# Attention on one core: score product ahead of the first value product, value bank copied first, mask and bias added on GpSimd in the sparse heads

## The chip, the cores and the metric

The kernel runs on 1 core of one Trainium2 chip. The metric is the time of one execution on the device in microseconds. Before the change the median of 3 runs is 1541.96 us (1541.03 to 1543.17).

## The reference

One layer of a hybrid encoder for 1,024 tokens plus 16 meta tokens (L = 1040), model width 1024, all in float32: a projection, two attention branches, a mixture of experts, norms. The change lies in the attention. Branch A has 8 dense heads, masked by chunks of 64 tokens. Branch B has 8 sparse heads: an indexer picks 256 keys for each query, and a relative bias (T5 buckets) is added before the softmax.

```python
# branch A, per block of 128 queries
s = (einsum('bqhd,bkhd->bhqk', qn, k_nope) + einsum('bqhr,bkr->bhqk', qr, k_rope)) * scale_a
s = where(cid[None, :] <= chunk_ids(pq)[:, None], s, NEG_INF)
o_a = einsum('bhqk,bkhd->bqhd', softmax(s), v_a)
# branch B, per block of 128 queries
score = einsum('bqh,bqhk->bqk', wb, relu(einsum('bqhd,bkd->bqhk', qib, k_i)))
_, idx = top_k(where(cid <= cq, score, NEG_INF), 256)
s = einsum('bqhd,bqkhd->bhqk', qb, gather(k_b, idx)) * scale_b
s = s + rel_bias[t5_bucket(idx - pq)]
s = where(valid, s, NEG_INF)
o_b = einsum('bhqk,bqkhd->bqhd', softmax(s), gather(v_b, idx))
```

The kernel gathers nothing: for the sparse heads it computes all scores of a block and adds a mask (0 or -1e30, bf16) that was made earlier from the indexer's scores.

## The kernel before

**Tiling.** The attention stage runs from about 547 to 899 us of the span. Queries come in 8 blocks of 128 rows; block i sees 16 + 128 (i + 1) keys, so its width WID[i] is 144, 272, 400, 528, 656, 784, 912 or 1040. Each of the 16 heads (0 to 7 dense, 8 to 15 sparse) is two super-steps: the even one handles blocks 0, 1, 2, 3 and the odd one blocks 4, 5, 7, 6 (`ORDER`), so the 1040 block comes before the 912 block. Super-step s holds block number g = 4 s + position; s >= 16 is sparse.

**Work of a block.** TensorE computes the scores (`qk`, f32 split in a high and a low part: three products in a dense head; in a sparse head one product of the identity with the mask, L1140, then two, L1143 and L1145), into one of two score areas in PSUM. VectorE takes the row maximum (`row_max`): in a dense head a reduction (L1285), in a sparse head one operation that adds the relative bias `tb`, writes the sum to `sbias` and gives the maximum (L1278), then a small negation (L1282). ScalarE takes the exponential (`exp`, L1227) into `px`.

**Work of a turn.** A super-step has turns, in an order written out by hand in `turns`: 5 (even) or 9 (odd) "p" turns, one for each tile of 128 keys; a "q" turn at index 5 that finishes the super-step before; and, in two of every four super-steps (s % 4 of 0 or 1), an "o" turn at index 2, which transposes finished outputs. In a "p" turn TensorE transposes `px` into a bank (L1187), ScalarE copies it rounded to `pH` (L1239), VectorE subtracts for the low part `pL` (L1302), and three turns later TensorE multiplies both with the values into the value bank, bank 7 (`pv`, L1203, L1204). `qk_after` says behind which turn the score product of a coming block is issued: index 0, 1, 3 of an even super-step (blocks 5, 7, 6 of the next), index 0, 1, 3, 5, 8 of an odd one (blocks 0 to 3 of the next, and block 4 of the one after). All engines keep this order: TensorE does turn, `pv`, `qk`; VectorE the subtraction, then `row_max`; ScalarE the copy, then the exponential of the block issued one turn earlier.

**The value bank.** It holds one super-step's sum. After its last `pv` (at turn index 2 of the next super-step, or 1 behind an even one without an "o" turn) ScalarE copies it to `oT` (L1251, semaphore `s_ot`); the first `pv` of the next super-step (turn index 3) waits for `s_ot`. In an "o" turn ScalarE also copies the output bank (L1243, to `OaT` or `ObT`), before the value bank.

**GpSimd** (`values`, `queries`, `keys`, `scaled`) splits values, queries and keys of coming heads in high and low parts and scales finished outputs (L1322), in this order: at odd s values, queries, scaled; at even s keys, scaled. `scaled(s - 1)` waits for VectorE's `otmp` (L1309, the "q" turn). **SP** loads queries, keys, the bias `tb` (two buffers) and values of the sparse heads; the load of `tb` for head h waits with `s_mx` for all maxima of head h - 2.

Of the kernel before, what the change touches and what calls it, by code (L numbers as in the profile page):

```python
# [88 lines left out]
def hybrid_layer(nc, a, out):  # L89

    ctx = ExitStack()
    with ctx:
# [905 lines left out]
        tb = [at(f"tb{k}", [P, L], F32, (R_Q + 8192, R_V + 8320)[k]) for k in range(2)]  # L998
        VR = [at(f"VR{k}", [P, 9, HD], F32, (R_Q + 12352, R_V + 12480)[k]) for k in range(2)]
# [79 lines left out]
        def bank_of(k):  # L1079
# [3 lines left out]
         s_vr) = map(sem, ["s_qk", "s_mx", "s_ml", "s_ex", "s_t", "s_ld", "s_rs", "s_pv", "s_ot", "s_qa", "s_rc",  # L1083
                           "s_om", "s_oe", "s_z", "s_vz", "s_hs", "s_hr", "s_vl", "s_vr"])

        with block() as blk:
            @blk.sync
            def _(sp):
                for h in range(H):
                    j, u, k, hh = h // 2, h % 2, h % 2, H + h  # L1090

                    sp.wait_ge(s_hr, 6 if h < 2 else 2 * (hh - 2) - 1)
                    for dup in range(2):
                        sp.dma_start(QR[k][64 * dup:64 * (dup + 1), :], qb_d[j, 64 * u:64 * (u + 1), :]
                                     ).then_inc(s_qr[k], 16)
                    if h >= 2:
                        sp.wait_ge(s_hr, 2 * (hh - 2))
                    for dup in range(2):
                        sp.dma_start(KR[k][64 * dup:64 * (dup + 1), :], kb_d[j, 64 * u:64 * (u + 1), :]
                                     ).then_inc(s_kr[k], 16)  # L1100
                    if h == 1:
                        sp.wait_ge(s_vr, 2 * H)
                    if h >= 2:
                        sp.wait_ge(s_mx, 8 * (h - 1))
                    sp.dma_start(tb[k][:, :], skewed[h]).then_inc(s_tb[k], 16)
                    if h >= 2:
                        sp.wait_ge(s_vr, 2 * (hh - 1))
                    c = slice(HD * h, HD * (h + 1))
                    sp.dma_start(VR[k][:, 0:8, :], vb_d[0:T, c].rearrange("(t p) c -> p t c", p=P)
                                 ).then_inc(s_vd[k], 16)  # L1110
                    sp.dma_start(VR[k][0:META, 8, :], vb_d[T:L, c]).then_inc(s_vd[k], 16)
                    if h == 1:
                        sp.wait_ge(s_hr, 2 * (H - 1))
                        for piece in range(2):
                            load_branch_weights(sp, piece, s_wb)

            @blk.tensor
            def _(pe):
                def qk(g):
# [17 lines left out]
                    if sparse(s):  # L1137
                        q = QS[hh % 2][:, own]
                        for lo, hi in parts:
                            pe.matmul(flat[:, o + lo:o + hi], identb[:, :], mask[:, OFF[i] + lo:OFF[i] + hi],  # L1140
                                      start=True, stop=False)
                        for lo, hi in parts:
                            pe.matmul(flat[:, o + lo:o + hi], q, kh[:, lo:hi], start=False, stop=False)  # L1143
# [65 lines left out]
                for k in range(len(turns)):  # L1209
                    turn(k)  # L1210
                    for n in pv_after[k]:
                        pv(n)
                    if k in qk_after:
# [3 lines left out]
            def _(act):  # L1217
# [14 lines left out]
                for k in range(len(turns)):  # L1232
# [7 lines left out]
                    elif kind == "o":  # L1240
                        act.wait_ge(s_t, k + 1)
                        to, j = (ObT, s // 4 - 4) if sparse(s) else (OaT, s // 4)
                        act.copy(to[:, j, 512 * (s % 2):512 * (s % 2 + 1)], bank_of(k)).then_inc(s_oe, 1)  # L1243
                    for before in pv_after[k]:
# [6 lines left out]
                        act.copy(oT[done % 2][:, :], ps[:, 7, :]).then_inc(s_ot, 1)  # L1251
                    if k - 1 in qk_after:
# [3 lines left out]
            def _(dve):  # L1256
# [4 lines left out]
                def row_max(g):  # L1261
# [8 lines left out]
                    if sparse(s):  # L1270
# [7 lines left out]
                        dve.tensor_tensor_reduce(sbias[g % 2][:, 0:w], flat[:, o:o + w], tb[h % 2][:, c:c + w],  # L1278
# [35 lines left out]
            def _(pool):  # L1314
# [55 lines left out]

                for k in range(2):
# [4 lines left out]
                for s in range(NSS):  # L1376
# [9 lines left out]
                    if s >= 1:  # L1386
                        scaled(s - 1)
                scaled(NSS - 1)
# [1089 lines left out]
```

## Time and profile before

| | us |
|---|---|
| median of 3 runs | 1541.96 |
| lowest, highest | 1541.03, 1543.17 |
| the profiled execution's own time | 1541.31 |
| its span | 1539.5 |
| TensorE (PE) busy | 1372.2 |
| VectorE (DVE) busy | 1031.2 |
| ScalarE (ACT) busy | 666.5 |
| GpSimd (POOL) busy | 420.2 |

The profile is one execution. PE is the matmul part of TensorE, PEld its loading of weights. A row of the timeline gives the start in us from the span's start, the duration, engine, line of the code, operation and the tiles it writes and reads; in brackets stands how long the engine had been idle and what ended that. "issue" means that nothing the profile shows released it.

### The profile page before, as it was taken

To read this page: it belongs to the slowest core of one execution; us is meant where nothing else is said; L and a number is where in the kernel's file an instruction comes from. 1 tells how busy PE (TensorE), PEld (TensorE's weight loads), DVE (VectorE), ACT (ScalarE), POOL (GpSimd) and SP (SyncE) were. 2 spreads that over 40 slices of the span, in tenths; PEclk is the share of its full clock that TensorE was granted. 3 is DMA by queue.
4 is the path that set the end of the run, shared out by engine and by line. 5 is a ranking of instruction groups with operands and counts; after the bars stand their busy time and mean duration, and the time that the engine had idled before them with its cause. 6 is when DMAs were issued, how large, how long until landed. Compare 5 with 4: busy or idle time off the path is not lost. (4 is left out here: it accounts for less than half of the span.)

```text
span 1539.5 us, 21819 instructions
## 1 busy us (share of the span) xinstructions
PE 1372.2 (89%) x7326; PEld 1120.2 (73%) x7327; DVE 1031.2 (67%) x1950; ACT 666.5 (43%) x1179; POOL 420.2 (27%) x476
## 2 busy tenths in 40 slices
PE   6989999999999989998888879999828999999950
PEld 4779788789989567777777768899726777777730
DVE  4458999999940856677777754433357777777727
ACT  5357323312211356666666651112106666666622
POOL 1100334412121044445544214200021233333213
PEclk9999999999999989999999989999858999999985
DMA  6040411132232003003442054222176999999718
GB/s 202 28 151 23 147 56 48 62 103 76 97 101 82 4 1 77 1 1 104 98 97 70 1 164 155 92 100 77 70 308 221 350 357 349 361 376 377 290 45 325
DMA packets 88702, 217.40 MB, mean 141 GB/s; under 512 B 24784, under 2 KB 49904, under 8 KB 76328
## 3 DMA queue, kind: packets, MB, share of 16 engines
q1 hardware_dynamic: 77200, 190.45, 35.7%
q0 software_dynamic: 9216, 16.80, 3.0%
q10 hardware_dynamic: 2200, 9.02, 1.5%
q8 instruction: 52, 0.85, 0.2%
q14 instruction: 34, 0.28, 0.1%
HBM read 193.05 MB, written 44.73 MB: 154 GB/s over the span
## 5 line engine op out<-in xcount | busy, mean ns | idle before, releaser
L421 PE MATMUL ps<-hHi,g_lead 128*128 128x512 f32 (+2 forms) x480 | 184.5, 384 | 7.8 <-DVE g_rest L818 6.6
L315 DVE TENSOR_SCALAR_CACHE_REDUCE mask<-score,cand 128x272 bf16<-128x272 f32 (+6 forms) x224 | 185.5, 892 | 4.6 <-DVE cand L334 4.4
L1302 DVE TENSOR_TENSOR pL<-ps,pH 128x512 fp32r<-128x512 f32 (+3 forms) x224 | 126.8, 573 | 89.2 <-ACT pH L1239 86.6
L2211 DVE TENSOR_TENSOR w_rest<-wgu,w_lead 128x1024 fp32r<-128x1024 f32 x128 | 155.9, 1222 | 45.1 <-ACT w_lead L2158 43.7
L422 PE MATMUL ps<-hLo,g_lead 128*128 128x512 f32 (+2 forms) x480 | 183.7, 383 | 0.0
L423 PE MATMUL ps<-hHi,g_rest 128*128 128x512 f32 (+2 forms) x480 | 182.5, 380 | 0.0
L2158 ACT CAST w_lead<-wgu 128x1024 fp32r<-128x1024 f32 x128 | 134.4, 1055 | 37.8 <-PE ps L2104 37.8
L1239 ACT CAST pH<-ps 128x512 fp32r<-128x512 f32 (+3 forms) x224 | 107.0, 492 | 70.9 <-PE ps L1187 70.7
L732 POOL TENSOR_TENSOR g_rest<-g_raw,g_lead 128x2048 fp32r<-128x2048 f32 x12 | 55.6, 4631 | 299.5 <-ACT g_lead L588 299.5
L2102 PE MATMUL ps<-w_lead,x_lead 128*128 128x512 f32 x256 | 114.0, 445 | 6.0 <-DVE w_rest L2211 6.0
L2124 PE MATMUL ps<-wd,hmT 128*128 128x512 f32 x256 | 115.3, 593 | 1.6 <-DVE hmT L2234 1.0
L1203 PE MATMUL ps<-pH,VS 128*128 128x512 f32 (+3 forms) x224 | 96.0, 429 | 17.7 <-issue 17.7
L421 PEld LDWEIGHTS ps<-hHi,g_lead 128*128 128x128 f32 x480 | 90.8, 189 | 24.8 <-issue 7.0
L423 PEld LDWEIGHTS ps<-hHi,g_rest 128*128 128x128 f32 x480 | 91.0, 190 | 16.6
L2104 PE MATMUL ps<-w_lead,x_rest 128*128 128x512 f32 x256 | 101.8, 398 | 0.0
L422 PEld LDWEIGHTS ps<-hLo,g_lead 128*128 128x128 f32 x480 | 90.8, 189 | 14.8
L2103 PE MATMUL ps<-w_rest,x_lead 128*128 128x512 f32 x256 | 100.8, 394 | 0.0
L2064 POOL DMA_INDIRECT ys_d<-ye,dk x32 | 32.3, 1010 | 213.1 <-DVE ye L2246 204.3
L2124 PEld LDWEIGHTS ps<-wd,hmT 128*128 128x128 f32 x256 | 46.2, 190 | 47.8 <-issue 47.8
L1204 PE MATMUL ps<-pL,VS 128*128 128x512 f32 (+3 forms) x224 | 79.5, 355 | 0.0
L1322 POOL TENSOR_TENSOR otok<-otmp,rec 128x256 f32<-128x256 f32 x32 | 19.6, 613 | 187.0 <-DVE otmp L1309 182.2
L619 ACT ACTIVATE stage<-ps 128x512 f32<-128x512 f32 x32 | 19.1, 598 | 112.0 <-PE ps L423 112.0
(349 smaller groups left out, 3433.2 us busy)
## 6 DMA issues: line engine op xcount, KB each, us to landing
wgu<-in_w_exp_gate SPq DMA_DIRECT2D x32, 1024.0 KB
wgu<-in_w_exp_up SPq DMA_DIRECT2D x32, 1024.0 KB
wd<-in_w_exp_down SPq DMA_DIRECT2D x32, 1024.0 KB, 11.7
g_raw<-in_w_in SPq DMA_DIRECT2D x16, 1024.0 KB, 5.6
gates_d<-stage SPq DMA_DIRECT2D x32, 256.0 KB, 2.0
gt<-gates_d SPq DMA_DIRECT2D x32, 256.0 KB, 3.1
rel_d<-rel_s ACTq DMA_DIRECT2D x1, 4672.0 KB
KR<-kb_d SPq DMA_DIRECT2D x16, 260.0 KB, 6.3
```

The source lines that it names most:

```text
L315: return dve.tensor_scalar(mask[:, OFF[i]:OFF[i + 1]], score[:, OFF[i]:OFF[i + 1]], thr, 0.0, op, ALU.add, accum_out=cnt[:, i:i + 1])
L421: pe.matmul(dst, x[0], y[0], start=(k == 0), stop=False)
L422: pe.matmul(dst, x[0], y[1], start=False, stop=False)
L423: return pe.matmul(dst, x[1], y[0], start=False, stop=(k == KT - 1))
L1239: act.copy(pH[n % RING][:, lo:512], bank_of(k)[:, lo:512]).then_inc(s_ld, 1)
L1302: dve.tensor_tensor(pL[n % RING][:, lo:512], bank_of(k)[:, lo:512], pH[n % RING][:, lo:512].bitcast(F32), ALU.subtract).then_inc(s_rs, 1)
L2102: pe.matmul(dst, xl[:, k, :], wl, start=(k == 0), stop=False)
L2103: pe.matmul(dst, xl[:, k, :], wr, start=False, stop=False)
L2104: mm = pe.matmul(dst, xr[:, k, :], wl, start=False, stop=(k == KT - 1))
L2124: mm = pe.matmul(ps[:, 5 + half, :], hmT[u % 2][:, k, :], wd[u][:, k, 512 * half:512 * (half + 1)], start=(k == 0), stop=(k == 1))
L2158: act.copy(w_lead[part][:, :, :, :], wgu[u][:, :, 2 * part:2 * part + 2, :]).then_inc(S["m_wl"], 1)
L2211: dve.tensor_tensor(w_rest[u][:, :, 2 * part:2 * part + 2, :], wgu[u][:, :, 2 * part:2 * part + 2, :], w_lead[part][:, :, :, :].bitcast(F3 ...
```

## The change

On TensorE, at a turn after which the first `pv` of a super-step stands (turn index 3), the score product is issued ahead of that `pv` instead of behind it. On ScalarE the copy of the value bank comes before the copy of the output bank. In the sparse heads the six blocks 2 to 7 (`JOINED`) have no mask product; GpSimd adds the block's mask (bf16) and relative bias (f32) into a tile `joined[i]` of its own, and VectorE's maximum reads that instead of `tb`. Blocks 0 and 1 stay as they are. The additions of super-step s + 2 stand at the end of GpSimd's work for super-step s: blocks 2 and 3 at even s, 4, 5, 7, 6 at odd s. SP's load of `tb` now waits for two maxima and all six additions of the head two before.

```diff
--- before.py
+++ after.py
@@ -996,6 +996,9 @@
         QS = [at(f"QS{k}", [P, T], F32R, R_Q + 4096 * k) for k in range(2)]
         sbias = [at(f"sbias{k}", [P, L], F32, R_V + 4160 * k) for k in range(2)]
         tb = [at(f"tb{k}", [P, L], F32, (R_Q + 8192, R_V + 8320)[k]) for k in range(2)]
+        JOINED = (2, 3, 4, 5, 7, 6)
+        joined = {i: at(f"tbm{i}", [P, WID[i]], F32, R_Q + 14656 + 4 * sum(WID[2:i])) for i in JOINED}
+        assert 14656 + 4 * sum(WID[2:]) <= 32768
         VR = [at(f"VR{k}", [P, 9, HD], F32, (R_Q + 12352, R_V + 12480)[k]) for k in range(2)]
         wbr = [at(f"wbr{k}", [P, 2, 4, 256], F32, R_K + 16640 + 8192 * k) for k in range(2)]
 
@@ -1080,8 +1083,8 @@
             return ps[:, bank_no[k], :]
 
         (s_qk, s_mx, s_ml, s_ex, s_t, s_ld, s_rs, s_pv, s_ot, s_qa, s_rc, s_om, s_oe, s_z, s_vz, s_hl, s_hr, s_vl,
-         s_vr) = map(sem, ["s_qk", "s_mx", "s_ml", "s_ex", "s_t", "s_ld", "s_rs", "s_pv", "s_ot", "s_qa", "s_rc",
-                           "s_om", "s_oe", "s_z", "s_vz", "s_hs", "s_hr", "s_vl", "s_vr"])
+         s_vr, s_jn) = map(sem, ["s_qk", "s_mx", "s_ml", "s_ex", "s_t", "s_ld", "s_rs", "s_pv", "s_ot", "s_qa", "s_rc",
+                           "s_om", "s_oe", "s_z", "s_vz", "s_hs", "s_hr", "s_vl", "s_vr", "s_jn"])
 
         with block() as blk:
             @blk.sync
@@ -1101,7 +1104,8 @@
                     if h == 1:
                         sp.wait_ge(s_vr, 2 * H)
                     if h >= 2:
-                        sp.wait_ge(s_mx, 8 * (h - 1))
+                        sp.wait_ge(s_mx, 8 * (h - 2) + 2)
+                        sp.wait_ge(s_jn, 6 * (h - 1))
                     sp.dma_start(tb[k][:, :], skewed[h]).then_inc(s_tb[k], 16)
                     if h >= 2:
                         sp.wait_ge(s_vr, 2 * (hh - 1))
@@ -1136,11 +1140,11 @@
                     kh, kl = KH[hh % 2], KL[hh % 2]
                     if sparse(s):
                         q = QS[hh % 2][:, own]
-                        for lo, hi in parts:
+                        for lo, hi in parts if i not in JOINED else ():
                             pe.matmul(flat[:, o + lo:o + hi], identb[:, :], mask[:, OFF[i] + lo:OFF[i] + hi],
                                       start=True, stop=False)
                         for lo, hi in parts:
-                            pe.matmul(flat[:, o + lo:o + hi], q, kh[:, lo:hi], start=False, stop=False)
+                            pe.matmul(flat[:, o + lo:o + hi], q, kh[:, lo:hi], start=i in JOINED, stop=False)
                         for lo, hi in parts:
                             mm = pe.matmul(flat[:, o + lo:o + hi], q, kl[:, lo:hi], start=False, stop=True)
                     else:
@@ -1208,9 +1212,12 @@
                     qk(g)
                 for k in range(len(turns)):
                     turn(k)
+                    opens = any(turns[n][2] == 0 for n in pv_after[k])
+                    if opens and k in qk_after:
+                        qk(qk_after[k])
                     for n in pv_after[k]:
                         pv(n)
-                    if k in qk_after:
+                    if not opens and k in qk_after:
                         qk(qk_after[k])
 
             @blk.scalar
@@ -1237,10 +1244,6 @@
                         if n >= RING:
                             act.wait_ge(s_pv, n - RING + 1)
                         act.copy(pH[n % RING][:, lo:512], bank_of(k)[:, lo:512]).then_inc(s_ld, 1)
-                    elif kind == "o":
-                        act.wait_ge(s_t, k + 1)
-                        to, j = (ObT, s // 4 - 4) if sparse(s) else (OaT, s // 4)
-                        act.copy(to[:, j, 512 * (s % 2):512 * (s % 2 + 1)], bank_of(k)).then_inc(s_oe, 1)
                     for before in pv_after[k]:
                         done = turns[before][1]
                         if turns[before] != last_tile(done):
@@ -1249,6 +1252,10 @@
                         if done >= 2:
                             act.wait_ge(s_t, turn_of[("q", done - 2, 0)] + 1)
                         act.copy(oT[done % 2][:, :], ps[:, 7, :]).then_inc(s_ot, 1)
+                    if kind == "o":
+                        act.wait_ge(s_t, k + 1)
+                        to, j = (ObT, s // 4 - 4) if sparse(s) else (OaT, s // 4)
+                        act.copy(to[:, j, 512 * (s % 2):512 * (s % 2 + 1)], bank_of(k)).then_inc(s_oe, 1)
                     if k - 1 in qk_after:
                         exp(qk_after[k - 1])
 
@@ -1275,7 +1282,11 @@
                             dve.wait_ge(s_tb[h % 2], 16 * (h // 2 + 1))
                             dve.wait_ge(s_vr, 2 * H)
                         c = P * (NB - 1 - i)
-                        dve.tensor_tensor_reduce(sbias[g % 2][:, 0:w], flat[:, o:o + w], tb[h % 2][:, c:c + w],
+                        add = tb[h % 2][:, c:c + w]
+                        if i in JOINED:
+                            dve.wait_ge(s_jn, 6 * h + JOINED.index(i) + 1)
+                            add = joined[i][:, :]
+                        dve.tensor_tensor_reduce(sbias[g % 2][:, 0:w], flat[:, o:o + w], add,
                                                  1.0, -3.0e38, ALU.add, ALU.max,
                                                  top[:, g % 2:g % 2 + 1]).then_inc(s_mx, 1)
                         dve.wait_ge(s_mx, g - 8 * H + 1)
@@ -1368,6 +1379,20 @@
                     pool.tensor_tensor(KL[k][0:rows_k, :], raw, KH[k][0:rows_k, :].bitcast(F32),
                                        ALU.subtract).then_inc(s_hr, 1)
 
+                def join(s):
+                    h, first = s // 2 - H, 4 * s - 8 * H
+                    if s == 2 * H:
+                        pool.wait_ge(s_hr, 2 * H)
+                    if s % 2 == 0:
+                        pool.wait_ge(s_tb[h % 2], 16 * (h // 2 + 1))
+                    for j, i in enumerate(ORDER[s % 2]):
+                        if i in JOINED:
+                            if h:
+                                pool.wait_ge(s_mx, first - 8 + j + 1)
+                            c = P * (NB - 1 - i)
+                            pool.tensor_tensor(joined[i][:, :], mask[:, OFF[i]:OFF[i + 1]], tb[h % 2][:, c:c + WID[i]],
+                                               ALU.add).then_inc(s_jn, 1)
+
                 for k in range(2):
                     pool.memset(VS[k][:, 8, :].bitcast(F32), 0.0).then_inc(s_vz, 1)
                 pool.wait_ge(s_vz, 2)
@@ -1385,6 +1410,8 @@
                         keys(hh + 1)
                     if s >= 1:
                         scaled(s - 1)
+                    if 2 * H <= s + 2 < NSS:
+                        join(s + 2)
                 scaled(NSS - 1)
 
         with block() as blk:
```

## Rows read from the trace of the kernel before

**Rows 1.** The page: busy time of each engine, its share of the span, and instructions.

```profile
PE 1372.2 (89%) x7326; PEld 1120.2 (73%) x7327; DVE 1031.2 (67%) x1950; ACT 666.5 (43%) x1179; POOL 420.2 (27%) x476
```

**Rows 2.** Stretches of two heads: dense, then sparse. Per engine: busy us (instructions), granted clock, DMA.

```profile
608.20:650.30 42.10, 38.48 (x269) 33.06 (x269) 29.45 (x52) 28.18 (x67) 20.57 (x21) 1.00 0.09 20
778.50:821.50 43.00, 37.60 (x253) 31.04 (x253) 31.37 (x84) 28.87 (x67) 20.62 (x21) 1.00 0.37 87
```

**Rows 3.** Timeline of sparse heads: start us, us, engine, line, operation; in brackets the wait before.

```profile
789.37 0.83 DVE L1278 CUSTOM_DVE_ANT_0 sbias<-ps,tb 128x656 f32<-128x656 f32 x1
...
810.56 0.83 DVE L1278 CUSTOM_DVE_ANT_0 sbias<-ps,tb 128x656 f32<-128x656 f32 x1
...
815.34 1.23 DVE L1278 CUSTOM_DVE_ANT_0 sbias<-ps,tb 128x1040 f32<-128x1040 f32 x1
...
816.96 0.47 PE L1203 MATMUL ps<-pH,VS 128*128 128x512 f32 x1 [0.93 <-issue]
...
818.46 0.56 DVE L1302 TENSOR_TENSOR pL<-ps,pH 128x384 fp32r<-128x384 f32 x1 [1.69 <-ACT pH L1239]
...
818.93 1.10 DVE L1278 CUSTOM_DVE_ANT_0 sbias<-ps,tb 128x912 f32<-128x912 f32 x1
...
820.26 1.05 ACT L1227 ACTIVATE pxb<-sbias,negm 128x912 f32<-128x912 f32 x1 [0.75 <-DVE negm L1282]
...
820.48 0.68 DVE L1309 TENSOR_REDUCE otmp<-ps 128x256 f32<-128x512 f32 x1
...
821.46 0.66 PE L1187 MATMUL ps<-con,pxb 128*128 128x128 f32 x4 [0.99 <-ACT pxb L1227]
```

**Rows 4.** Timeline of dense heads.

```profile
610.79 0.62 PE L1187 MATMUL ps<-con,pxa 128*128 128x128 f32 x4
...
611.99 0.47 PE L1203 MATMUL ps<-pH,VS 128*128 128x512 f32 x1 [0.57 <-issue]
...
624.00 1.24 DVE L1285 TENSOR_REDUCE negm<-ps 128x1 f32<-128x1040 f32 x1 [0.41 <-PE ps L1154]
...
627.46 1.11 DVE L1285 TENSOR_REDUCE negm<-ps 128x1 f32<-128x912 f32 x1 [0.25 <-PE ps L1154]
...
644.64 0.28 PE L1204 MATMUL ps<-pL,VS 128*128 128x128 f32 x1
...
644.78 0.58 ACT L1243 COPY OaT<-ps 128x512 f32<-128x512 f32 x1 [0.21 <-PE ps L1191]
```

**Rows 5.** Timeline, TensorE, the 912 block's three products and what follows.

```profile
796.38 0.56 PE L1140 MATMUL ps<-mask,identb 128*128 128x456 bf16 x2
...
797.60 0.27 PE L1187 MATMUL ps<-con,px 128*128 128x128 f32 x1
```

**Rows 6.** Groups of instructions of GpSimd in two sparse heads: busy us, mean ns.

```profile
L1368 POOL TENSOR_TENSOR KL<-KR,KH 128x1040 fp32r<-128x1040 f32 x2 | 4.8, 2424 | 0.2
...
L1339 POOL TENSOR_TENSOR VS<-VR,VS 128x512 fp32r<-128x512 f32 x2 | 2.6, 1284 | 0.2
L1366 POOL CAST KH<-KR 128x1040 fp32r<-128x1040 f32 x2 | 2.1, 1052 | 0.0
```

**Rows 7.** Timeline of GpSimd in a sparse head.

```profile
778.25 0.61 POOL L1322 TENSOR_TENSOR otok<-otmp,rec 128x256 f32<-128x256 f32 x1 [9.33 <-DVE otmp L1309]
778.81 0.61 POOL L1336 CAST VS<-VR 128x512 fp32r<-128x512 f32 x1
...
782.28 2.39 POOL L1355 TENSOR_TENSOR QS<-QR,QS 64x1024 fp32r<-64x1024 f32 x1
...
799.98 0.61 POOL L1322 TENSOR_TENSOR otok<-otmp,rec 128x256 f32<-128x256 f32 x1 [9.60 <-DVE otmp L1309]
```

**Rows 8.** VectorE's negation, all of them, and one beside GpSimd's work.

```profile
L1282 DVE TENSOR_SCALAR negm<-top x64: 153/154/156, 716.3 to 884.9; 128x1 f32<-128x1 f32 x64
...
809.50 2.41 POOL L1368 TENSOR_TENSOR KL<-KR,KH 128x1040 fp32r<-128x1040 f32 x1
...
811.43 0.15 DVE L1282 TENSOR_SCALAR negm<-top 128x1 f32<-128x1 f32 x1
```

## The prediction

> **What bounds the kernel now.** I began with the page: TensorE is busy for 89% of the span and GpSimd for 27% [rows 1]. Shares of a whole span say little of one stage, so the second view is the table of stretches, cut at the start of an odd super-step, which repeats every two heads. Two dense heads take 42.1 us with TensorE busy 38.48; two sparse heads take 43.0 us with TensorE 37.60, VectorE 31.37, ScalarE 28.87 and GpSimd 20.62 [rows 2]. TensorE is the busiest everywhere and still idles 5.4 us in two sparse heads. Whether it decides is a question of order, not of shares, so the third view is the timeline, read backwards from one wait to what ended it.
>
> In a sparse head I start from the transposes that open an odd super-step: at 821.46 TensorE had waited 0.99 us for the exponential of block 6 (912 columns). That exponential (820.26) waited for VectorE's negated maximum, the row maximum (818.93) stood right behind the low-part subtraction (818.46), which had waited 1.69 us for ScalarE's high-part copy, and that copy comes, in ScalarE's order, behind the exponential of the 1040 block, whose maximum ran at 815.34 [rows 3]. So it goes on: maximum, exponential, copy, subtraction, next maximum, handed between VectorE and ScalarE, each in its written order. TensorE enters the chain once a head, with the four transposes at 821.46. Its score product is not in it: it waited 0.93 us at 816.96 for the value bank's copy, and the row maximum was still held by the subtraction.
>
> In a dense head the maximum is a plain reduction, with no negation of its own, and TensorE comes into the chain: the maximum of the 1040 block had waited 0.41 us for TensorE at 624.00, and that of the 912 block 0.25 us at 627.46 [rows 4].
>
> **Part 1: the score product ahead of the first value product.** At turn index 3 of every super-step the score product goes before the value product that waits for s_ot. In the dense heads TensorE stood 0.57 us at 611.99, between an odd super-step with an output turn and the even one behind it [rows 4]. The transposes ahead of that wait started at 610.79 and need about 0.4 us to issue, so the score product can start at about 611.2, up to 0.79 us earlier. The next place where the chain is seen waiting for TensorE is the 1040 block's maximum, which has 0.41 us of such a wait: the gain is between 0.41 and 0.79. I take 0.65, because copies and subtractions before it wait for TensorE too. The 912 block's maximum gains its 0.25 as well, since its product now ends early. Together 0.90 in each of the three dense pairs that have this (super-steps 5/6, 9/10, 13/14), and 0.25 once at super-step 2: -2.95 us. In the sparse heads the same swap fills a 0.93 us idle and gives nothing, because the work behind it was not waiting for TensorE. No DMA is moved by this part.
>
> **Part 2: the value bank copied before the output bank.** On ScalarE the order is output copy, value copy, exponential. The two copies cost the same in either order, unless the value bank is not ready. At an even dense super-step with an output turn the last value product ends at 644.64 + 0.28 = 644.92 while the output copy could start at 644.78 [rows 4]. ScalarE now stands for about 0.17 us, and what is queued behind it are both copies and the 1040 exponential, hence the chain. Three such places: +0.5 us. The dense net of parts 1 and 2 is -2.45 us, or between -1.7 and -2.9 with the bounds above.
>
> **Part 3: six mask products out, six additions in.** Removed from TensorE: the bf16 products of mask and identity in the six blocks above 272 columns, 4,320 columns a head. The three products of the 912 block (2,736 columns) started at 796.38 and the next transposes at 797.60 [rows 5], 0.446 ns a column; so 1.93 us a head, 15.4 us over eight heads. By the chain above this is worth nothing: VectorE's reduction has the same width, ScalarE's exponential the same, and the products were not late. VectorE gets one more wait per maximum, which costs nothing while the maximum stands behind a subtraction.
>
> Added to GpSimd: six additions a head, bf16 plus f32 to f32. No such operand pair is in the trace. Nearest are the f32 subtractions: 1.284 us for 512 columns and 2.424 for 1040 [rows 6], so 0.18 us and 2.16 ns a column. That gives 1.04, 1.32, 1.59, 1.87, 2.42 and 2.15 us for 400, 528, 656, 784, 1040 and 912, 10.4 us a head. GpSimd goes from 10.3 to 20.7 of 21.5 us. Below, a one-input cast of 1040 columns took 1.05 us [rows 6], so the additions can't be under 43% of my price. Above, the dearest f32 work of two inputs is this same row, and a conversion could add to it; I allow 20% more and take the f32 price.
>
> Now the order on GpSimd. Inside an even super-step a scaling starts at 799.98, right after VectorE's otmp. Behind it now come 400 and 528 (0.56 for the scaling, 2.26 with the 0.05 overlap of each), then values and queries, which ran from 778.81 to 782.28 + 2.39 = 784.67, 5.86 us, a gap of 0.07, the second scaling 0.56, then 656, 1.59 us, and 0.06 to VectorE [rows 7]. The joined 656 block is there at 799.98 + 10.96 = 810.94. The row maximum that reads it ran at 810.56 [rows 3]: 0.38 late. In the other kind of odd super-step (with an output turn) GpSimd starts at 778.25, the block is there at 789.21, and the maximum ran at 789.37: in time by 0.16. After the 656 block, 1040 was needed 4.8 us later (815.34) and comes 4.2 after it; 912 and the keys' split end 9.9 us after it, and otmp for the next scaling ended at 820.48 + 0.68, 10.6 after it [rows 3]. So four of eight odd super-steps are late by 0.38: +1.5 us. Queued behind the late maximum is the whole VectorE-ScalarE chain.
>
> The DMA side: SP's load of the relative bias waited for the last maximum of the head two before; it now waits for two maxima and six additions of it, which end some 2 us earlier, and queries and keys of the next head, behind it on SP, are needed a head later. Nothing.
>
> VectorE and GpSimd side by side: 64 negations took 153 to 156 ns each, and the one at 811.43 ran in the middle of a 2.41 us GpSimd subtraction begun at 809.50 [rows 8]. The Trainium skill (SBUF - State Buffer, Who interferes with whom) says that VectorE's f32 single-input operations in their two-port modes and GpSimd lock one another out for a whole instruction. By that rule GpSimd at 96% would hold up each negation; by the row it would not. The row decides, so the sum has nothing for it.
>
> **The sum.** -2.45 + 1.5 = -0.9 us. The profiled execution took 1541.31 us for its span of 1539.5; the median of the runs is 1541.96, 0.65 above it, and the difference carries over: 1541.1 us.
>
> **Rivals.**
> *A: the additions are in time.* With a price 25% under mine nothing is late: -2.45, at most -2.9, 1539.1 to 1539.5 us.
> *B: GpSimd sets the pace (the other side).* Before a 656 block 1,584 columns of additions stand, after it 2,736. For each 10% on their price the first makes 0.34 us, with slacks of -0.38 and 0.16, and the second 0.59 with a slack of about 0.65. At +20% two heads lose 1.06 + 0.52 + 2 x 0.53 = 2.6 us, ten over eight heads: 1541.96 - 2.45 + 10.5 = 1550 us. From about +13% the kernel is slower by over 0.2%. For it speaks that GpSimd is left with 0.8 us a head; against it that the price of two f32 inputs is steady in the trace.
> *C: TensorE decides after all.* Then the mask columns count in full: -15.4 us, 1526.6 us, and the filled waits on top. For it: TensorE is busiest; against it: rows 3. The Trainium skill (Perfetto Trace Analysis, Identifying the Most-Contended Engine) says to improve the engine with the highest occupancy first; by that rule this would be the result.
> *D: the lock.* If each of eight negations a head waited half a mean addition (0.87 us), 7 us a head: 1597 us.
>
> **Chances.** Forecast 0.47, A 0.20, B 0.22, C 0.07, D 0.04. What this measurement can tell is 0.2%, 3.1 us. A ends close above that bound and a dense gain a little larger crosses it: Faster gets half of A, all of C and 0.08 of the forecast's own spread, 0.25; slower gets B but its mild 0.05, D and 0.01 of the forecast, 0.22; within, 0.53. The range leaves out C, D and the far end of B: 1537.5 to 1549.0 us.
>
> **What would show it.** Right: two sparse heads stay at 42.5 to 44 us though TensorE's busy time falls by 3 to 4; before every second 656 maximum VectorE waits 0.3 to 0.5 us for GpSimd; the value product's waits are gone in both halves; two dense heads take about 41.4 us. Wrong: sparse heads well under 42 us (then C), GpSimd additions over 1.15 times my prices (B), negations over 0.2 us apart from the work ahead (D), or dense heads unchanged.

## The result, and the profile after

The changed kernel takes 1546.48 us (median of 8 runs, 1544.02 to 1549.28) beside 1542.07 us (8 runs) for the kernel before on the same chip: a ratio of 1.0028, 95% interval 1.0018 to 1.0037. It is slower by 4.4 us; the forecast was 0.9 us faster. Measured again later it came out at 1.0016 (1.0007 to 1.0025), so the loss is 2.5 to 4.4 us. The profiled execution took 1546.49 us, its span is 1544.6.

The page, in its busy row and two of its groups (busy us, mean ns, idle before):

```profile
PE 1367.7 (89%) x7230; PEld 1116.0 (72%) x7231; DVE 1029.8 (67%) x1950; ACT 664.8 (43%) x1179; POOL 493.2 (32%) x524
...
L1313 DVE TENSOR_TENSOR pL<-ps,pH 128x512 fp32r<-128x512 f32 (+3 forms) x224 | 126.8, 572 | 92.8 <-ACT pH L1246 90.9
...
L1393 POOL TENSOR_TENSOR tbm<-mask,tb 128x400 f32<-128x400 bf16 (+5 forms) x48 | 74.0, 1573 | 0.0
```

GpSimd has the 48 additions, 74.0 us. TensorE's busy time should have fallen by the 15.4 us of the mask products and fell by 4.5 only [rows 1]: its other instructions must have become longer somewhere. That is the first sign of what went wrong.

The additions by size, and VectorE's negation (count: least, median, greatest ns):

```profile
L1393 POOL TENSOR_TENSOR tbm<-mask,tb 128x1040 f32<-128x1040 bf16 x8 | 17.6, 2196 | 0.0
...
L1393 POOL TENSOR_TENSOR tbm<-mask,tb 128x656 f32<-128x656 bf16 x8 | 11.6, 1448 | 0.0
...
L1393 POOL TENSOR_TENSOR tbm<-mask,tb 128x400 f32<-128x400 bf16 x8 | 7.6, 950 | 0.0
```

```profile
L1293 DVE TENSOR_SCALAR negm<-top x64: 153/154/156, 714.3 to 887.3; 128x1 f32<-128x1 f32 x64
```

The additions are some 10% under their price, the negations exactly what they were [rows 8]. Neither is the loss.

Now the table of stretches: a dense pair, and four sparse heads, each cut at VectorE's reciprocal of an odd super-step (us, busy us of each engine, granted clock, DMA):

```profile
629.40:670.68 41.28, 38.53 (x268) 32.84 (x268) 29.05 (x53) 28.46 (x66) 20.57 (x21) 1.00 0.00 1
```

```profile
711.95:733.90 21.95, 17.63 (x116) 14.80 (x117) 16.08 (x47) 13.98 (x33) 19.75 (x17) 0.99 0.24 60
733.90:756.54 22.64, 18.92 (x114) 15.38 (x112) 15.60 (x43) 14.15 (x33) 19.27 (x17) 0.93 0.36 87
756.54:778.96 22.42, 18.81 (x117) 16.54 (x118) 15.64 (x42) 14.23 (x33) 19.69 (x17) 0.92 0.34 81
778.96:800.18 21.22, 17.45 (x113) 13.90 (x111) 15.53 (x43) 14.14 (x33) 19.22 (x17) 1.00 0.34 83
```

The dense pair is 0.82 us shorter than before [rows 2], about as forecast. The sparse heads differ among themselves: where the granted clock is 1.00 a head takes 21.22 us, where it is 0.92 or 0.93 it takes 22.4 to 22.6, with 1.2 to 1.5 us more of TensorE for the same work. (The first row is the first sparse head, which takes 21.94 us in the kernel before too.) Short stretches around the places show how low it goes:

```profile
733.00:738.00 5.00, 4.44 (x26) 4.29 (x27) 2.51 (x9) 2.41 (x8) 4.59 (x6) 0.66 0.69 157
756.00:761.00 5.00, 4.44 (x26) 4.39 (x27) 2.57 (x10) 2.90 (x8) 4.71 (x7) 0.66 0.53 120
778.00:783.00 5.00, 4.30 (x33) 3.81 (x34) 2.87 (x11) 3.82 (x12) 4.52 (x6) 1.00 0.67 154
```

A mean of 0.66 over 5 us is 3.4 us at half the clock (1.2 in place of 2.4 GHz) and the rest at full. There are four such falls in this kernel's sparse heads and none in the kernel before. The timeline shows what TensorE did ahead of two of them, and at a like place without a fall (778.63):

```profile
731.51 0.33 PE L1208 MATMUL ps<-pL,VS 128*128 128x384 f32 x1
733.56 1.11 PE L1191 MATMUL ps<-con,pxb 128*128 128x128 f32 x4 [1.72 <-ACT pxb L1234]
734.32 0.56 PE L1207 MATMUL ps<-pH,VS 128*128 128x256 f32 x1
...
756.56 0.65 PE L1191 MATMUL ps<-con,pxb 128*128 128x128 f32 x4 [2.29 <-ACT pxb L1234]
...
778.63 0.66 PE L1191 MATMUL ps<-con,pxb 128*128 128x128 f32 x4 [1.72 <-ACT pxb L1234]
779.04 0.36 PE L1207 MATMUL ps<-pH,VS 128*128 128x256 f32 x1
```

At 733.56 the four opening transposes take 1.11 us and at 778.63, with the same wait ahead, 0.66; the product behind them 0.56 and 0.36. The wait itself is what the new order made: before, this place had waits of 0.99 [rows 3] and 1.22 us, head by head in turn, and the value product one of 0.93 us [rows 3]:

```profile
800.34 0.66 PE L1187 MATMUL ps<-con,pxb 128*128 128x128 f32 x4 [1.22 <-ACT pxb L1227]
```

Now the value product doesn't wait, and the opening waits 1.72 and 2.3 us by turns. TensorE's waits in a dense pair say the same of its half: the 1.9 us that the value products waited before are gone, and ScalarE's wait for transposes went from 10.6 to 6.9 us. After (us in total, times, longest):

```profile
ACT pH L1246 <- PE ps L1191: 6.9, 13, 1.2
...
PE ps L1191 <- ACT pxa L1234: 2.7, 3, 1.3
...
ACT oT L1254 <- PE ps L1208: 0.4, 1, 0.4
```

The kernel before had, in the same kind of stretch (us in total, times, longest):

```profile
ACT pH L1239 <- PE ps L1187: 10.6, 15, 1.1
...
PE ps L1203 <- issue: 1.9, 3, 0.7
```

### The profile page after: what moved, and what is told of

Its sections match the earlier page's. It is cut to its first block and busy times, and to the rows that moved or that the text cites. A ratio compares the mean times of both kernels' runs of the same rounds, so it can differ in the third digit from the quotient of the medians.

```text
span 1544.6 us, 21689 instructions
## 1 busy us (share of the span) xinstructions
PE 1367.7 (89%) x7230; PEld 1116.0 (72%) x7231; DVE 1029.8 (67%) x1950; ACT 664.8 (43%) x1179; POOL 493.2 (32%) x524
## 5 line engine op out<-in xcount | busy, mean ns | idle before, releaser
L1393 POOL TENSOR_TENSOR tbm<-mask,tb 128x400 f32<-128x400 bf16 (+5 forms) x48 | 74.0, 1573 | 0.0
```

## The experiments

The theory: the new order joins two waits of TensorE into a longer one, the granted clock falls behind it, and each fall costs about a microsecond ("clock" below). Rivals: GpSimd's additions hold the chain up, and the loss lies in stages outside the attention. Each kernel ran on the chip beside the kernel before. Twelve of them, in four groups.

**1. The parts by themselves.** e1_order has the swap on TensorE and on ScalarE, and keeps the mask products; e2_join has the additions and keeps the old order; e3_zero is the changed kernel with a zero weight times the mask in the six blocks; e4_maskout is the kernel before without the mask products in the six blocks and with nothing in their place, so its scores there lack the mask.

```
e1  + opens = any(turns[n][2] == 0 for n in pv_after[k])   # and the output copy behind oT
e2  the diff without its hunks on pv_after/qk_after and on the output copy
e3  + pe.matmul(flat[..], zerob, mask[..], start=True)     # zerob: 128 x 128 zeros
    - pe.matmul(flat[..], q, kh[..], start=i in JOINED)
    + pe.matmul(flat[..], q, kh[..], start=False)
e4  - for lo, hi in parts:                                 # the mask product
    + for lo, hi in parts if i < 2 else ():
```

> Parts 1 and 2 alone: the two new orders, with the mask products kept on TensorE and nothing on GpSimd. Theory 'clock' (the loss comes from TensorE standing so long in one piece before an odd super-step that its clock is granted at half for 3.4 us): two dense heads take 41.3 us as in the changed kernel (42.1 before). In the sparse heads TensorE keeps its 15 us of mask products, so its longest wait stays near 1.9 us and the granted clock 1.00; time about 2.5 us under the kernel before. If the clock falls here too, 1 to 1.5 us are lost at each fall and the gain shrinks to nothing. Rival 'GpSimd' (the additions are what costs): the same 2.5 us gain, and no loss anywhere. Rival 'elsewhere' (the difference of the changed kernel lies outside the attention): 2 to 5 us slower here as well, with the attention stage shorter.

> Part 3 alone: additions on GpSimd, six mask products out, both old orders. 'Clock': TensorE's waits stay split between the first value product (about 1.3 us) and the odd super-step (about 1.4), so the granted clock stays at 1.00 in the sparse heads or falls less often than the four times of the changed kernel; sparse pairs of heads 42.9 to 43.3 us, time within 1.5 us of before. 'GpSimd': the additions cost here what they cost in the changed kernel, some 4 to 5 us. 'Elsewhere': slower by 2 to 5 us with the attention stage unchanged.

> The changed kernel, but TensorE still runs a product for the mask in the six blocks, with a zero weight tile in place of the identity, so that it adds nothing: GpSimd and VectorE do all that they do in the changed kernel, and TensorE has its old load. 'Clock': granted clock 1.00 through the sparse heads, pairs of sparse heads 42.9 us against 44.3, time 2 to 3 us under the kernel before. 'GpSimd': as slow as the changed kernel, about 4.4 us over the one before. If the clock falls although the load is back, it is the new order and not the missing products that makes it fall.

> The kernel before with the mask products of the six blocks left out and nothing in their place: the sparse heads attend to all keys of those blocks, so this is a time only. It takes 15 us of columns from TensorE and adds no work. If TensorE's load bound the stage, about 15 us less. By the chain read in the trace of before: no gain, within 1 us. 'Clock': like the run with part 3 alone in its falls of the clock, since TensorE's stream is the same.

Measured: 1.0000 (0.9989 to 1.0011), 1.0012 (1.0003 to 1.0021), 1.0005 (0.9996 to 1.0014) and 1.0010 (1.0000 to 1.0019). No part alone is the loss. The new order comes out even, though its dense heads are faster: it has five falls. TensorE's mask products taken away with nothing in their place (e4), 15.4 us by the prediction's count, make the kernel no faster, and shorten the eight sparse heads by 1.1 us together (the table in group 3): TensorE's load hardly sets the pace. And with that load back in place (e3) the falls do not go: three. So they are not simply a matter of how much TensorE has to do. Of what e2 and e4 lose, 2.3 and 1.7 us lie in the last stage of the kernel, to which I come at the end ("Outside the attention").

**2. Where the order acts, and the wait filled.** e5_dense has the new order in the dense heads only. e7_fill is the changed kernel and e8_orderfill is e1_order, both with four bf16 products of 512 columns on TensorE ahead of the wait that opens an odd super-step of the sparse heads. They write the bank that the transposes overwrite. e9_before is the kernel before again.

```
e5  - opens = any(turns[n][2] == 0 for n in pv_after[k])
    + opens = any(turns[n][2] == 0 and turns[n][1] < 2 * H for n in pv_after[k])
e7, e8, in turn(k), where kind == "p", t == 0, s odd and sparse:
    + for _ in range(4):
    +     pe.matmul(bank[:, :], identb[:, :], mask[:, 0:512], start=True, stop=True)
      pe.wait_ge(s_ex, 4 * s + 4)
```

> The new order of products and copies in the dense heads alone; sparse heads as before. Theory clock (the new order gathers TensorE's waits of a sparse head into one of 1.7 to 2.3 us ahead of the odd super-step, behind which the granted clock falls from 2.4 to 1.2 GHz for 3.4 us at times): dense part 2.5 to 3.3 us shorter, sparse part 172 to 173 us with no fall or one, kernel 2 to 3 us faster than before (ratio 0.998 to 0.9987). Theory that the order gives nothing anywhere because ScalarE and VectorE pace both halves: ratio 1.000, dense pairs 42.1 us as before. Theory elsewhere (the time is lost in stages outside the attention whatever is changed): the sum over the attention falls by 2.5 to 3 us and the span does not.

> The changed kernel with four idle bf16 products of 512 columns (about 0.9 us) on TensorE ahead of the wait that opens each odd super-step of the sparse heads; they write a bank that the transposes behind them overwrite, and the result is not touched. Theory clock: the wait is split, the falls in the sparse heads go from four to one or none, sparse heads take 21.2 to 21.6 us each (part 172 us or less instead of 176.7), kernel 3 to 6 us faster than the changed one, ratio to before 0.997 to 0.9995. Theory GpSimd (the additions slow the chain): added products on TensorE change nothing, ratio 1.002 to 1.004, sparse heads as in the changed kernel. Theory that TensorE's total load matters and not where it lies: as with the zero-weight products, which were 2,160 bf16 columns a super-step against 2,048 here in every second one: three falls or so, ratio 1.000 to 1.001.

> The new order alone (mask products kept, no additions on GpSimd) with the same four idle products ahead of the same wait. Theory clock: no fall or one in the sparse heads instead of five, sparse heads 21.2 us each, part about 171 us; kernel 3 to 5 us faster than before (ratio 0.997 to 0.998). If this and the changed kernel with the same filling come out within 0.1% of each other, moving the mask's sum to GpSimd is worth nothing by itself, as the chain of ScalarE and VectorE says. Theory GpSimd: this one 2 us or more faster than the other.

> The kernel before once more, unchanged. Theory clock: no fall or at most one in the sparse heads, sparse part 172 to 173.5 us, ratio 1.000. Theory elsewhere: the profile of before that was shown had a short tail by chance; the stretch behind the attention, 653.2 us there and 655.9 to 656.8 us in the changed kernel and the four others, comes out at 655 to 657 us here too.

Measured: e5 0.9981 (0.9972 to 0.9990), e7 0.9994 (0.9985 to 1.0003), e8 0.9983 (0.9974 to 0.9991), e9 1.0003 (0.9994 to 1.0012). Two stretches of e7 and the opening of one:

```profile
754.49:776.19 21.70, 18.23 (x120) 15.16 (x122) 15.63 (x43) 13.91 (x33) 19.70 (x17) 1.00 0.38 88
776.19:797.40 21.21, 18.24 (x116) 14.20 (x115) 15.51 (x43) 14.14 (x33) 19.22 (x17) 1.00 0.36 87
```

```profile
775.23 0.81 PE L1191 MATMUL ps<-mask,identb 128*128 128x512 bf16 x3 [1.09 <-DVE pL L1319]
775.88 0.63 PE L1197 MATMUL ps<-con,pxb 128*128 128x128 f32 x4
```

Work that computes nothing, put into the wait, makes the kernel faster: against the changed kernel e7 gains 4.3 us by the ratios (0.9994 against the mean of 1.0028 and 1.0016). There is no fall left in the sparse heads, and the longest wait is 1.35 us. (The trace holds three of the four products at 775.23; the first is missing from it.) The heads are 21.2 and 21.7 us by turns, and nothing about the additions changed. The rival of GpSimd is refuted for the greater part of the loss; what is left of it is in the 21.7, to which I come in group 4.

**3. The dose.** e6_sparse has the new order in the sparse heads only (the condition of e5 turned round), e10_half is e7 with two idle products in place of four, e11_after is the changed kernel again.

```
e6   + opens = any(turns[n][2] == 0 and turns[n][1] >= 2 * H for n in pv_after[k])
e10  + for _ in range(2):                                  # 4 in e7
```

> The new order in the sparse heads alone, mask products kept, no additions; dense heads as before. Theory clock (the wait of 1.7 to 2.3 us ahead of the odd super-step brings the falls): three to five falls of 3.4 us in the sparse heads, part 174.5 to 176 us, kernel 1 to 4 us slower than before, ratio 1.0007 to 1.0025; with the 0.9981 of the dense heads alone it multiplies to the 1.000 of both. Theory that nothing in the sparse heads depends on the order, as the prediction had it: ratio 1.000 and sparse part 172.3 us.

> The changed kernel with two idle products of 512 columns (about 0.45 us) ahead of the wait that opens each odd super-step of the sparse heads, half of what removed all falls. If the length of the one gathered wait decides: waits of 1.4 to 1.9 us are left, falls in between (one to three in the sparse heads), time between the 1541.8 with four products and the 1546.5 without, 1542.5 to 1545 us, ratio 1.000 to 1.0015. If any work at all in the wait is enough: as with four, no fall, ratio 0.999 to 1.000.

> The changed kernel once more, unchanged. Theory clock: falls of 3.4 us in the sparse heads again, three to five of them, not all at the same heads; sparse part 175 to 178 us, ratio 1.002 to 1.0035. If the four falls of the first profile were chance: none or one here, and the time of the kernel would have to come from elsewhere, such as a stretch outside the attention that is 3 us longer than before.

Measured: e6 1.0014 (1.0005 to 1.0023), e10 1.0002 (0.9993 to 1.0011), e11 1.0016. With e5's 0.9981, e6 multiplies to 0.9995, e1's result within its interval: what the order gains in the dense heads it loses in the sparse ones. All kernels together, by the longest wait of TensorE in the sparse heads (falls are stretches of 3.4 us at the half clock there, the last super-step included; the sparse part runs from the eighth to the sixteenth reciprocal of an odd super-step, and leaves out one fall each of e1, e3 and e6):

```
kernel                   longest wait   falls   sparse part   ratio
before, e9 (two profiles)   1.22 us      0, 0    172.3, 172.4   1, 1.0003
e5  order, dense only       1.22         0       172.3          0.9981
e8  order, 4 products       1.35         0       171.2          0.9983
e7  changed, 4 products     1.35         0       171.9          0.9994
e12 e7, early addition       1.35        0       171.3          0.9985
e4  mask products out       1.47         2       171.3          1.0010
e2  additions, old order    1.48         1       172.5          1.0012
e10 changed, 2 products     1.78         2       173.5          1.0002
e3  changed, zero product   2.22         3       173.9          1.0005
e6  order, sparse only      2.25         3       173.3          1.0014
e1  order                   2.24         5       175.8          1.0000
changed, e11 (two profiles) 2.31, 2.30   4, 5    176.7, 176.7   1.0028, 1.0016
```

Of the 22 falls in the kernels with the new order, every one begins between 0.3 us before and 1.5 us after the end of such an opening wait, each of 1.7 us or more; not every such wait is followed by one (4 and 5 of 8 in the two profiles of the changed kernel). The three falls of e2 and e4 begin behind two waits of 0.78 and 0.94 us close to one another, ahead of the opening, and cost little: the stretches from reciprocal to reciprocal that they lie in take 22.12, 21.42 and 21.58 us, and 21.94, 21.42 and 21.48 in the kernel before. The Trainium skill (TensorE: Matmul & The Clock Gate, Part 1) says that a hardware monitor sets the engine's clock by how busy it was of late; the rows above agree, and they show such falls in a stream in which TensorE is busy for over 80% of the time.

The price of a fall behind the opening wait: e1, e3, e6, e10 and the two profiles of the changed kernel have 19 falls inside the sparse part and are together 19.8 us longer there than e8 or e7, whichever has the same additions: 1.04 us each. Four or five make 4.2 to 5.2 us.

**4. The late addition.** e7's heads of 21.7 us, beside e8's of 21.4 and 21.5. VectorE's maximum of the 656 block and GpSimd ahead of it, in e7:

```profile
763.86 0.89 DVE L1319 TENSOR_TENSOR pL<-ps,pH 128x384 fp32r<-128x384 f32 x2 [0.66 <-ACT pH L1252]
764.93 0.84 DVE L1295 CUSTOM_DVE_ANT_0 sbias<-ps,tbm 128x656 f32<-128x656 f32 x1 [0.19 <-POOL tbm L1399]
```

```profile
762.75 0.61 POOL L1339 TENSOR_TENSOR otok<-otmp,rec 128x256 f32<-128x256 f32 x1
763.32 3.09 POOL L1399 TENSOR_TENSOR tbm<-mask,tb 128x656 f32<-128x656 bf16 x2
```

The block's addition starts at 763.32 and, at the 1448 ns that one takes, ends at about 764.77; the maximum starts at 764.93 after 0.19 us of waiting for it. In e8, which has no additions, the maximum starts 0.08 us before the subtraction ends (765.18 + 0.89), so the loss is 0.27 us. In e7 VectorE waits so in three of the eight sparse heads (0.19, 0.12 and 0.12 us), and these heads are 0.28, 0.20 and 0.20 us longer than e12's. In the changed kernel itself it waits 0.12 us twice in one profile and not at all in the other. e8's rows:

```profile
765.18 0.89 DVE L1311 TENSOR_TENSOR pL<-ps,pH 128x384 fp32r<-128x384 f32 x2 [0.66 <-ACT pH L1248]
765.99 0.83 DVE L1287 CUSTOM_DVE_ANT_0 sbias<-ps,tb 128x656 f32<-128x656 f32 x1
```

e12_early is e7 with the addition of that block moved ahead of the value and query splits:

```
  if s % 2 == 1:
+     if 2 * H <= s + 2 < NSS:
+         join(s + 2, (0,))        # the 656 block; the other three stay where they were
      if hh < HH:
          values(hh)
```

> The changed kernel with the four idle products, and on GpSimd the addition of each odd super-step's first block (656 columns) moved ahead of the value and query splits of its turn, so that it is done long before the maximum that reads it. Theory that the late block costs 0.27 us in every second sparse head (10.44 against 10.17 us behind the head's start, beside the kernel without additions): the 21.7 us heads become 21.4 to 21.5, sparse part 170.8 to 171.2 us instead of 171.9, ratio 0.998 to 0.9992 against 0.9994. Theory that the maximum is held by something else (the width, VectorE's extra wait instruction): heads stay at 21.70, sparse part 171.9. If the additions hold up the splits instead: heads longer than 21.7 and waits for QS or VS on TensorE.

Measured: 0.9985 (0.9976 to 0.9994), sparse part 171.3 us, the heads at 21.42 and 21.49. Its rows:

```profile
764.60 0.89 DVE L1319 TENSOR_TENSOR pL<-ps,pH 128x384 fp32r<-128x384 f32 x2 [0.66 <-ACT pH L1252]
765.40 0.83 DVE L1295 CUSTOM_DVE_ANT_0 sbias<-ps,tbm 128x656 f32<-128x656 f32 x1
```

```profile
776.64:819.37 42.73, 36.33 (x236) 29.40 (x237) 31.14 (x86) 28.15 (x66) 39.04 (x33) 1.00 0.37 89
```

The same stretch of two heads in e8:

```profile
777.23:819.94 42.71, 39.06 (x260) 31.87 (x261) 31.12 (x86) 28.34 (x66) 20.60 (x22) 1.00 0.36 87
```

The wait is gone, and nothing else became late, with GpSimd busy for 39.0 of 42.7 us. e12 against e8 is the changed split of the mask's work with both faults mended: 0.9985 against 0.9983, nothing. So the simplest version that beats both kernels is e5: the new order in the dense heads alone, 0.9981. (Its sparse heads are 1.1 us longer than those of e8 and e12, and its last stage 1.5 to 2.0 us shorter; see "Outside the attention".)

## Why the prediction was wrong, step by step

**What failed.** The step is "In the sparse heads the same swap fills a 0.93 us idle and gives nothing, because the work behind it was not waiting for TensorE." That the work behind was nearly never waiting is true. But a wait that is filled on an engine off the chain doesn't vanish: TensorE comes to its next wait so much earlier. The 0.93 us went to the opening of the odd super-step, 0.99 and 1.22 became 1.72 and 2.3, and behind that the granted clock fell four or five times a run. The prediction has no term for the granted clock at all, although the page and every stretch show it; [rows 2] read 1.00 in both halves, and I took that as given for the changed kernel. A fall makes TensorE, busy for over 80% of a head's time at the full clock, late for the chain: +1.04 us each, +4.2 to +5.2 us. The forecast's range reached to 1549.0 for another reason (rival B), so that the measured time lies inside it is luck. The falls are the greater part of the loss and not all of it: the sum also has no term for the stages behind the attention, and the last of them is about 1.9 us longer ("Outside the attention" below).

The same step was wrong in a smaller way too. At a steady clock the swap does gain in the sparse heads: every second head takes 21.22 us in place of 21.50, 171.2 against 172.3 us for the part (e8), 1.1 us. Taking the mask products out without the swap (e4) gives the same 1.1 us, and both together (e12) no more than one.

**What held.** Part 1, dense: 0.73 us a pair with part 2's cost in it; measured 0.82 in the pair [rows 2] and 2.9 us for the kernel (e5), at the edge of the range given (-1.7 to -2.9). What was sized too small is the term of 0.25 at super-step 2. The granted clock also falls at the start of the attention in every kernel, once or twice, for 3.4 or 6.8 us, and by it the stretch from the first to the second reciprocal of an odd super-step takes 20.5 to 23.9 us; with falls of the same length there it takes 22.96 us in e9 and 22.00 in e5, 0.96 less. Part 2: +0.17 at the value copy, and ScalarE's copy now waits 0.4 us there where the output copy waited 0.21 [rows 4].

Part 3, the removal: worth nothing beside the swap, as said (e12 against e8), and 1.1 us without it (the sparse heads of e4). Rival C is refuted. Its 15.4 us of TensorE's busy time were too many: in two heads e12 has 36.33 us where e8, with the products, has 39.06, so 10.9 us over eight heads. In the changed kernel the four falls put 5 to 6 us of busy time back (1.2 to 1.5 us each), which leaves a saving of about 5 us; the page's busy time fell by 4.5.

Part 3, the additions: 9.4 us a head in place of 10.4. The step "the joined 656 block is there ... 0.38 late" and "four of eight odd super-steps" had the right place, and a number of heads and a size somewhat too large: three heads, 0.20 to 0.28 each, +0.7 us in e7 in place of +1.5, and two heads or none in the changed kernel. With the additions at what they took (3.60 us for the three ahead of the maximum, in place of 3.95) the working would have given 0.38 - 0.35 = 0.03. Of the difference to 0.27 I can place 0.10: from the addition's end to the maximum's start it is 0.16 us (group 4), where I had allowed 0.06. Rival A had its price wrong (25% under mine, measured 9%), and its conclusion, that nothing is late, is wrong for e7. Rival B's step of 0.34 us for each 10% counts the columns alone; with the fixed part of three additions it is 0.40.

Rival D, the lock: the negations are unchanged at 153 to 156 ns with GpSimd busy for 85 to 91% of a head; the measurement decides against the rule as the prediction had applied it.

The sum of all that was in it was -0.9 us. e7, the changed kernel with the falls prevented, measured 0.9994, which is -0.9 us too (-2.3 to +0.5), but that is partly luck: the late block cost less than the forecast had and the swap gained more, and against them stands a term that the forecast lacked.

**Outside the attention.** From the terms in the attention (dense -2.9, sparse base 171.9 - 172.3 = -0.4, falls +4.7) the changed kernel should lose 1.4 us, and loses 2.5 to 4.4. The rest lies behind the attention, where no code was changed: from the last reciprocal to the end 656.0 and 655.7 us in two profiles of the changed kernel, 653.2 and 654.3 in two of the kernel before. About 2 us of this are in the last stage, which begins when SP issues its first load of `fa`. SP's second issue there, before and in the changed kernel, and VectorE's first addition, which waits for it:

```profile
1498.43 0.43 SPq L2412 DMA_DIRECT2D fb<-ys_d  x1
...
1502.87 1.23 DVE L2451 TENSOR_TENSOR fa<-fa,fb 128x1024 f32<-128x1024 f32 x1 [16.24 <-DMA fb<-ys_d]
```

```profile
1501.62 1.59 SPq L2439 DMA_DIRECT2D fb<-ys_d  x1
...
1507.93 1.23 DVE L2478 TENSOR_TENSOR fa<-fa,fb 128x1024 f32<-128x1024 f32 x1 [18.28 <-DMA fb<-ys_d]
```

In the changed kernel the queue for instructions (q8 on the page), which loads the code, moves one packet of 16 KB, of 1.2 us, at the very time of the long issue. The kernel before has its last such packet 37 us ahead of this stage. The view of 1501.5 to 1501.7 us in the changed kernel, by queue, has nothing but this packet (packets, MB, share of 16 engines):

```profile
q8 instruction: 1, 0.02, 37.7%
```

All profiles fall in two groups by this. In before, e9, e5, e6, e3 and e1 the packet is 37 us ahead, and the last stage takes 41.4 to 41.9 us. In the changed kernel, e11, e2, e4, e7, e8, e10 and e12 it comes 0.4 to 0.7 us behind SP's first load, and the stage takes 43.0 to 44.1 us (the changed kernel 43.4 both times). So the changed kernel has +1.9 us there, and the terms add up to +3.3 us. e7 has the same (43.2), so that its gain over the changed kernel is not touched by it. e8 differs from e1 by 32 products on TensorE alone and is in the other group. That it is the amount of code that moves the packet is my reading; no run changed the code and nothing else.

**What stays open.** Between the last reciprocal and the last stage the profiles spread by 4 us (610.9 to 614.8), which goes with none of the edits that I can see; the changed kernel (612.6, 612.3) and the kernel before (611.8, 612.8) don't differ there beyond it. One kernel's profile says nothing of how often a fall or such a spread comes, and the -2.9 us of the dense heads has an interval of 1.4 us to either side. Nor is it settled why one wait of 1.72 us is followed by a fall and another is not.

## What to carry to other kernels

Filling a wait of an engine that is off the chain buys nothing where the chain is, and lengthens that engine's next wait; on TensorE, look at how long the longest wait becomes and at the granted clock of the stretch behind it. When TensorE's busy time falls by less than the work taken away, look for a lower clock before anything else. A reordering that pays in one phase should be tried in that phase alone: here it is the difference between 0.9981 and 1.0000. And when differences of 0.1% count, compare the stages that the change doesn't touch as well: here a load of code that fell into another place goes with some 1.9 of the 2.5 to 4.4 us.

## What the runs showed of the hardware that I had not expected

- The granted clock fell from 2.4 to 1.2 GHz for 3.4 us at a time in a phase in which TensorE is busy for over 80% of the time, behind single waits of 1.7 to 2.3 us, and in two kernels behind shorter waits close together. Before each fall the clock had been full.
- Some 0.9 us of products that compute nothing, put into that wait, took away all falls of the sparse heads and made the kernel 4.3 us faster; half as many left two. A fall behind that wait cost 1.04 us; the three that came ahead of it (e2, e4) cost about 0.2 us or less.
- GpSimd's addition of a bf16 and an f32 operand takes 950 ns for 400 columns and 2196 for 1040, 1.95 ns a column, less than the 2424 ns of the subtraction of two f32 operands of 1040 columns [rows 6].
- A packet of 16 KB on the queue for instructions (1.2 us) fell together with a DMA issue of SP that took 1.59 us in place of 0.43, at the start of the last stage. In the eight profiles that have it there, the stage took 43.0 to 44.1 us, in the other six 41.4 to 41.9.
